# Second self-attention's distance term on VectorE, spatial gate's norm on ScalarE, convolution one step later

## The chip, the cores and the metric
The kernel runs on one core of one Trainium2 chip. The metric is the time of one execution in microseconds (us) on the device: the median of three runs of the kernel before is 791.27 us (791.15 to 791.55). TensorE does the matrix products, VectorE and ScalarE the elementwise work, GpSimd some small work and a few loads, and SyncE issues the weight loads.

## The reference
Two transformer layers on 256 tokens of width 1024, in fp32. The second one holds what is changed:

```
h = rms_norm(x, pre_mix_g);  za, zb, zc = split(h @ w_in)
ya = spatial_gating(gelu(za)):
     u, v = halves;  v = layer_norm(v, ln_g, ln_b)
     mixed[t] = sum_s tril(w_s)[t, s] * v[s] + b_s[t]      (4 heads of 64, chunks of 128 tokens)
     ya = u * mixed
yb = attention of 8 heads of 64: softmax(q.k / 8 - slope_h * (t - s)), causal, slope_h = 2^-(h+1), h = 0..7
yc = silu(group_norm(causal depthwise convolution of 31 taps of a * sigmoid(g)))
x = x + rms_norm(concat(ya, yb, yc) @ w_out, post_mix_g)
```
After it come a cross attention to 256 memory tokens and a feed-forward block. (256 tokens are one block of the block-sparse attention, so all keys up to the query's own are used.)

## The kernel before
**Units.** All weights come in 248 units of 256 rows by 512 columns (512 KB), in a ring of four. For each unit ScalarE makes a rounded high part (`hi`, line 538), VectorE the rest as a low part (`lo`, line 1004), and TensorE multiplies in three passes (lines 1847 to 1849, 1912 to 1915). `after(u)` on ScalarE and VectorE prepares unit u + 4; the high part waits until TensorE has ended unit u and so freed the slot. Each engine's program is written out by hand, in order, and the engines meet at semaphores; nothing is reordered.

**The stretch of the change.** After the first layer's feed-forward block the units come in this order: MEM_K0 (memory keys), GLU2 (convolution input), Q2, K2 (queries and keys), MEM_K1 (2 units), GELU2 (gate, 4), V2 (values, 4), MEM_V0 (memory values, 4), OUT2 (output projection, 8), MEM_V1. The small work of attention, gate and convolution is hung between the units from MEM_K1 on: `follow(step)` exists on TensorE, ScalarE and VectorE, step 0 and 1 are the MEM_K1 units, 2 to 5 GELU2, 6 to 9 V2, 10 to 13 MEM_V0, 14 to 21 OUT2. On TensorE a step's work comes after its unit; on ScalarE after the `after` of its unit; on VectorE ahead of it.

**Attention.** Four pairs of heads, scores at steps 0, 1, 6 and 7. Each pair has two banks. `scores` (line 2112) makes the products of queries and keys (line 2117) and then, in the second attention, adds the distance term by four more products per pair: a diagonal of slopes times the matrix of negative distances with the mask in it (line 2122). `take_maxima` on VectorE reduces the banks (line 1157) and negates (1161); `exponentials` on ScalarE reads the banks (line 612) in the following step; `reciprocals` on VectorE (line 1166) and `normalize` on ScalarE (line 621) follow; `turn_prob` transposes on TensorE (line 2145) at steps 4, 5, 11 and 13. The first attention uses `take_scores` instead: VectorE adds a scalar and a mask to the bank and writes SBUF (line 1141), then takes the maxima there (1148).

**Spatial gate.** `gate_norm` (step 8, VectorE, line 1483) takes the row statistics, GpSimd the power, `gate_scale` (step 9, VectorE, lines 1492 to 1495) subtracts, scales, and applies the norm's weight and bias rows, six instructions of 256 columns. TensorE mixes at step 12 (line 2411), VectorE adds the bias row b_s (line 1504), multiplies by u and splits.

**Convolution.** 62 taps on VectorE (line 1471) are spread behind the units from Q2 on; then TensorE averages over the groups (`conv_center`, step 13), VectorE subtracts, ScalarE squares (13), TensorE sums (14), VectorE copies (14), GpSimd takes the power, TensorE spreads the scale (16), VectorE multiplies (16), ScalarE does Silu (17), VectorE splits into high and low part (18). OUT2's units use the attention's first half (units 0, 1), the gate (2, 3), the attention's second half (4, 5) and the convolution (6, 7: they wait for `yc`).

**Ahead of feed-forward one.** `turn_normed` transposes the normalised rows of token tile 0 and 1, with the two units MEM_KE between.

Of the kernel before, what the change touches and what calls it, by code (L numbers as in the profile page):

```python
# [32 lines left out]
SMALL_LOADS = 7  # L33
# [3 lines left out]
           ("conv_gn_g_2", 2), ("conv_gn_b_2", 2))  # L37
# [4 lines left out]
W_DW, W_CONV, C_POOL, C_BDW, C_GNG, C_GNB = (COL_AT[n] for n in (  # L42
    "w_dw_2", "conv_w", "pool_scale", "b_dw_2", "conv_gn_g_2", "conv_gn_b_2"))
# [206 lines left out]
class Signals:  # L250


    def __init__(self, new):
# [18 lines left out]
        self.ones_ok, self.slopes_ok = new("ones_ok"), new("slopes_ok")  # L272
# [37 lines left out]
        self.gate_var, self.gate_rstd, self.v_normed = new("gate_var"), new("gate_rstd"), new("gate_v_normed")  # L310
        self.gate_mix_ps, self.gate_mixed, self.ya = new("gate_mix_ps"), new("gate_mixed"), new("ya")
# [10 lines left out]
class Memory:  # L322


    def __init__(self, nc, ctx):
# [40 lines left out]
        self.slopes = sb("slope_diagonals", [NH, P], F32R)  # L366
        self.dist_r = sb("neg_dist_rounded", [S], F32R)
# [23 lines left out]
        self.ln_rows = sb("gate_ln_rows", [2, 256])  # L391
# [134 lines left out]
def act_program(nc, t, m, s):  # L526
# [79 lines left out]
    def exponentials(a, g, soft, b=None):  # L606
        act.wait_ge(*a.max.at(g + 1))
        _, negmx, rsum = m.pair_stats(g)
        for e, tt, c0, c1 in parts():
            i = 2 * e + tt  # L610
            logits = soft[:, e, c0:c1] if b is None else bank[b + e][:, c0:c1]
# [218 lines left out]
    act.wait_ge(s.ident_ok, 1)  # L830
    act.wait_ge(s.dist_ok, 1)
# [22 lines left out]
    def follow(step):  # L854
        a = s.att2
        if step == 9:
            normalize(a, 2, m.soft2[2])
        if step in (1, 2, 8, 9):
            g = (1, 2, 8, 9).index(step)
            exponentials(a, g, m.soft2[g], pair_bank(g))  # L860
# [132 lines left out]
def dve_program(nc, m, s):  # L993
# [141 lines left out]
    def take_scores(a, g, b0, b1, soft):  # L1135

        dve.wait_ge(*a.scores.at(g + 1))
        mx, negmx, _ = m.pair_stats(g)
        for e, tt, c0, c1 in parts():
            keys = slice(P, S) if tt == 0 else slice(0, S)  # L1140
            ins = dve.scalar_tensor_tensor(out=soft[:, e, c0:c1], in0=bank[b1 if e else b0][:, c0:c1],
                                           scalar=m.cum8[:, tt, 2 * g + e:2 * g + e + 1], in1=m.mask[:, keys],
                                           op0=ALU.add, op1=ALU.add)
# [6 lines left out]
        dve.tensor_scalar(negmx, mx, -0.125, None, ALU.mult).then_inc(a.max.sem, 1)  # L1150

    def take_maxima(a, g, b):

        dve.wait_ge(*a.scores.at(g + 1))
        mx, negmx, _ = m.pair_stats(g)
        for tt, (c0, c1) in enumerate(CUTS):
            ins = dve.tensor_reduce(mx.rearrange("p (e t) -> p e t", t=NT)[:, :, tt], m.banks[:, b:b + 2, c0:c1], AX.X,
                                    ALU.max)
        ins.then_inc(a.logits.sem, 1)
        dve.wait_ge(*a.logits.at(g + 1))  # L1160
        dve.tensor_scalar(negmx, mx, -0.125, None, ALU.mult).then_inc(a.max.sem, 1)
# [100 lines left out]
    def attention1(step):  # L1262
        if step == 1:
            rows = slice(0, 2 * NH)
            dve.wait_ge(s.cum_ps, 1)
            dve.wait_ge(s.consts_ok, 1)
            dve.tensor_scalar(m.cum8[:, :, :].rearrange("p a h -> p (a h)"), bank[6][:, 0:2 * NH], -1.0, None,
                              ALU.mult).then_inc(s.cum_out, 1)
            own.then(dve.tensor_copy(m.key_round[rows, :], bank[7][rows, 0:S]))
            dve.scalar_tensor_tensor(out=m.key_sums[rows, :], in0=as_f32(m.key_round[rows, :]),  # L1270
                                     scalar=m.low_rows[rows, :], in1=bank[7][rows, 0:S], op0=ALU.mult,
                                     op1=ALU.add).then_inc(s.key_sums, 1)
            dve.wait_ge(s.cum_out, 1)
            dve.wait_ge(s.mask_ok, 1)
        for g, at in enumerate(ATT1_AT):
            if step == at:
                take_scores(s.att1, g, 4, 5, m.soft1[g])
            if step == at + 2:
                reciprocals(s.att1, g)
# [92 lines left out]
    keys_lo(0, 4)  # L1372

# [101 lines left out]
    for j in range(2 * RING):  # L1475
        after(Q2 + j)
        conv_taps(5)

# [9 lines left out]
    def gate_scale():  # L1488
        dve.wait_ge(s.gate_rstd, 1)
        for tt in range(NT):  # L1490
            v = m.vg[:, tt, :]
            own.then(dve.tensor_scalar(v, v, m.gate_stat[:, 2 * tt:2 * tt + 1], m.gate_stat[:, 6 + tt:7 + tt],
                                       ALU.subtract, ALU.mult))
            own.then(dve.tensor_tensor(v, v, m.ln_rows[:, 0, :], ALU.mult))
            dve.tensor_tensor(v, v, m.ln_rows[:, 1, :], ALU.add).then_inc(s.v_normed, 1)
            dve.wait_ge(s.v_normed, tt + 1)

    def gate_mix():
        dve.wait_ge(s.gate_mix_ps, 1)
        dve.wait_ge(s.u_ok, 1)  # L1500
        for tile in range(2):
            for tt in range(NT):
                c = slice(tt * P, tt * P + P)
                ins = dve.tensor_tensor(m.ya[:, tile, c], bank[2][:, tile * S + tt * P:tile * S + tt * P + P],
                                        m.bs_row[:, tile, :], ALU.add)
# [8 lines left out]
    def follow(step):  # L1514
        a = s.att2
        if step in (0, 1, 6, 7):
            g = (0, 1, 6, 7).index(step)
            take_maxima(a, g, pair_bank(g))
# [4 lines left out]
        if step == 9:  # L1523
            gate_scale()
# [9 lines left out]
        if step == 13:  # L1534
            dve.wait_ge(s.conv_mean_ps, 1)
            dve.tensor_tensor(conv2, conv2, bank[5][:, :], ALU.subtract).then_inc(s.conv_cen, 1)
        if step == 14:
            dve.wait_ge(s.conv_var_ps, 1)
            dve.tensor_copy(stat[:, 8:16], bank[5][:, 0:8]).then_inc(s.conv_var, 1)
        if step == 16:  # L1540
            dve.wait_ge(s.conv_scale_ps, 1)
            dve.tensor_tensor(conv2, conv2, bank[5][:, :], ALU.mult).then_inc(s.conv_scaled, 1)
        if step == 18:
# [4 lines left out]
    for j in range(2):  # L1548
        follow(j)
        after(MEM_K1 + j)  # L1550
        conv_taps(1)
    for j in range(RING):
# [4 lines left out]
        conv_taps(4)  # L1557
    for j in range(RING):
# [4 lines left out]
        conv_taps((1, 1, 1, 0)[j])  # L1563
    for j in range(RING):
        follow(10 + j)
        after(MEM_V0 + j)
        conv_taps((1, 0, 0, 0)[j])
# [83 lines left out]
def pool_program(nc, t, m, s):  # L1651
# [94 lines left out]
    load_small(m.ln_rows[:, 0, :], t["gate_ln_g_2"].broadcast_to([P, 256]))  # L1746
    load_small(m.ln_rows[:, 1, :], t["gate_ln_b_2"].broadcast_to([P, 256]))
# [86 lines left out]
def pe_program(nc, m, s):  # L1834
# [277 lines left out]
    def scores(a, g, banks, forget=False):  # L2112


        for e, tt, c0, c1 in parts():
            rows = slice(64 * e, 64 * e + 64)
            mm = pe.matmul(bank[banks[e]][:, c0:c1], m.qT[rows, g, tt * P:tt * P + P], m.kT[rows, g, 0:c1 - c0],  # L2117
                           start=tt == 0, stop=False, skip_group_check=True)
        if forget:
            return  # L2120
# [228 lines left out]
    def early_keys(tt):  # L2349
# [4 lines left out]
        if tt:  # L2354
            free[2] = s.mem_keys, 1

# [33 lines left out]
    def scores2(g):  # L2390
        claim(*pair_banks(g))
        if g == 0:
            pe.wait_ge(s.q2_out, 2)
            pe.wait_ge(s.k2_out, 2)
            pe.wait_ge(s.slopes_ok, 1)
# [49 lines left out]
    def follow(step):  # L2445
# [12 lines left out]
        if step == 13:  # L2458
            conv_center()
        if step == 14:  # L2460
            conv_norm()
        if step == 16:
# [173 lines left out]
```

## Time and profile before
| | |
|---|---|
| median of 3 runs | 791.27 us |
| profiled execution | 791.54 us, span 790.1 us |
| TensorE busy | 775.7 us, 98% |
| VectorE busy | 567.8 us, 72% |
| ScalarE busy | 434.8 us, 55% |
| GpSimd busy | 87.9 us, 11% |
| TensorE's share of the chain that ended last | 91% |

The profile is one execution. Busy time is the share of the span in which an engine had an instruction running. TensorE's products are pipelined, so one of 395 ns is followed by the next after 230 ns; in the chain of waits each stands with the time until the next. The chain follows back from the last instruction to what released each step.

### The profile page before, as it was taken

What the parts mean: (1) busy time and instruction counts of PE and PEld (TensorE: products, weight loads), DVE (VectorE), ACT (ScalarE), POOL (GpSimd) and SP (SyncE); (2) the same over time, 40 slices, a digit from 0 to 9 for tenths busy, and PEclk for the clock granted to TensorE, in tenths of its full rate; (3) what the DMA queues carried; (4) which work ended last, traced back from release to release, by engine and by line L of the source; (5) the groups of instructions that cost most, each with busy time, mean ns of one, the idle gap of its engine ahead of it and who ended that gap; (6) DMA issues with size and microseconds to landing.
All of it is one profiled execution on the core that took longest, in us unless ns stands there. A gap on an engine that the chain in (4) does not pass through costs nothing.

```text
span 790.1 us, 11526 instructions
## 1 busy us (share of the span) xinstructions
PE 775.7 (98%) x4516; PEld 675.0 (85%) x4516; DVE 567.8 (72%) x754; ACT 434.8 (55%) x653; POOL 87.9 (11%) x141
## 2 busy tenths in 40 slices
PE   6999999999999999999999999999999999999997
PEld 5999877788898888888899997889988988888885
DVE  4986999859787567676667997657657666665664
ACT  5555477675665444444466476656646644444452
POOL 5033990000010000000020000101001100000001
PEclk9999999999999999999999999999999999999999
DMA  9998988954457686865556654446433766666651
GB/s 320 367 285 311 359 293 287 349 163 161 133 162 238 197 300 195 266 216 183 166 185 211 181 159 141 146 148 213 149 95 105 215 199 196 188 188 189 190 179 54
DMA packets 84630, 163.61 MB, mean 207 GB/s; under 512 B 5457, under 2 KB 15889, under 8 KB 84577
## 3 DMA queue, kind: packets, MB, share of 16 engines
q1 hardware_dynamic: 82656, 157.31, 62.0%
q10 hardware_dynamic: 1424, 4.81, 1.6%
q0 software_dynamic: 496, 0.76, 0.4%
q8 instruction: 36, 0.59, 0.3%
q14 instruction: 18, 0.14, 0.0%
HBM read 161.81 MB, written 1.05 MB: 206 GB/s over the span
## 4 chain that ended last, share of the span: by engine, by line
PE 91%; DVE 3%; issue 1%; ACT 1%; DMA 1%; SPq 1%; POOL 1%; ACTq 0%; DVEq 0%; POOLq 0%
PE bank L1847 19%; PE bank L1848 19%; PE bank L1849 19%; PE bank L1912 13%; PE bank L1915 7%; PE bank L1860 2%; PE bank L1866 2%; PE bank L1862 2%; DVE ada_acc L1034 1%; DMA raw_ring<-in_w_in 1%; PE bank L1965 1%; PE bank L2540 1%; PE bank L2117 1%; SPq L492 1%; DVE lo_ring L1004 1%
## 5 line engine op out<-in xcount | busy, mean ns | idle before, releaser
L1004 DVE TENSOR_TENSOR lo_ring<-raw_ring,hi_ring 128x1024 fp32r<-128x1024 f32 x248 | 305.6, 1237 | 152.1 <-ACT hi_ring L538 151.4
L538 ACT CAST hi_ring<-raw_ring 128x1024 fp32r<-128x1024 f32 x248 | 259.6, 1052 | 248.8 <-PE bank L1849 148.8
L1847 PE MATMUL bank<-hi_ring,branch_hi 128*128 128x512 f32 x352 | 139.0, 395 | 0.0
L1848 PE MATMUL bank<-lo_ring,branch_hi 128*128 128x512 f32 x352 | 137.2, 390 | 0.0
L1849 PE MATMUL bank<-hi_ring,branch_lo 128*128 128x512 f32 x352 | 137.0, 389 | 0.0
L1912 PE MATMUL bank<-h_hi_lo,hi_ring 128*128 128x512 f32 x448 | 111.8, 391 | 0.0
L1912 PEld LDWEIGHTS bank<-h_hi_lo,hi_ring 128*128 128x128 f32 x448 | 81.3, 189 | 15.1
L1849 PEld LDWEIGHTS bank<-hi_ring,branch_lo 128*128 128x128 f32 x352 | 66.1, 188 | 14.0
L1847 PEld LDWEIGHTS bank<-hi_ring,branch_hi 128*128 128x128 f32 x352 | 66.2, 188 | 13.9 <-issue 0.8
L1848 PEld LDWEIGHTS bank<-lo_ring,branch_hi 128*128 128x128 f32 x352 | 66.2, 188 | 13.4 <-issue 0.5
L1847 PE MATMUL bank<-h_hi_lo,hi_ring 128*128 128x256 f32 x240 | 69.0, 288 | 0.0
L1848 PE MATMUL bank<-h_hi_lo,hi_ring 128*128 128x256 f32 x240 | 67.9, 283 | 0.0
L1849 PE MATMUL bank<-h_hi_lo,lo_ring 128*128 128x256 f32 x240 | 67.9, 283 | 0.0
L1915 PEld LDWEIGHTS bank<-h_hi_lo,lo_ring 128*128 128x128 f32 x448 | 61.1, 190 | 4.4
L1847 PE MATMUL bank<-hi_ring,h_hi_lo 128*128 128x512 f32 (+1 forms) x160 | 63.5, 397 | 0.4 <-DVE post_rows L1112 0.4
L1915 PE MATMUL bank<-h_hi_lo,lo_ring 128*128 128x256 f32 x448 | 62.5, 282 | 0.0
L1849 PE MATMUL bank<-hi_ring,h_hi_lo 128*128 128x512 f32 (+1 forms) x160 | 60.9, 380 | 0.0
L1848 PE MATMUL bank<-lo_ring,h_hi_lo 128*128 128x512 f32 (+1 forms) x160 | 60.8, 380 | 0.0
L1683 POOL TENSOR_SCALAR stat<-stat 128x1 f32<-128x1 f32 x10 | 2.6, 261 | 440.5 <-ACT gates L597 440.5
L1847 PEld LDWEIGHTS bank<-h_hi_lo,hi_ring 128*128 128x128 f32 x240 | 46.0, 192 | 0.4 <-issue 0.2
L1848 PEld LDWEIGHTS bank<-h_hi_lo,hi_ring 128*128 128x128 f32 x240 | 46.0, 192 | 0.2
L1849 PEld LDWEIGHTS bank<-h_hi_lo,lo_ring 128*128 128x128 f32 x240 | 46.0, 191 | 0.0
(301 smaller groups left out, 1179.3 us busy)
## 6 DMA issues: line engine op xcount, KB each, us to landing
raw_ring<-in_w_ff SPq DMA_DIRECT2D x128, 512.0 KB, 3.7
raw_ring<-in_w_in SPq DMA_DIRECT2D x64, 512.0 KB, 4.6
raw_ring<-in_w_out SPq DMA_DIRECT2D x16, 512.0 KB, 3.4
raw_ring<-in_w_xkv SPq DMA_DIRECT2D x16, 512.0 KB, 3.6
mem_v<-in_w_ada SPq DMA_DIRECT2D x13, 512.0 KB, 5.3
mem_k<-in_w_ada SPq DMA_DIRECT2D x11, 512.0 KB, 4.9
ada_ring<-in_w_ada SPq DMA_DIRECT2D x8, 512.0 KB, 6.9
raw_ring<-in_w_branch SPq DMA_DIRECT2D x8, 512.0 KB, 3.8
```

What stands on the lines that cost most here:

```text
L492: sp.dma_start(dst[:, :, i * S:i * S + S] if a < ADA_FIRST else dst.rearrange("p k n -> p (k n)"), src).then_inc(s.ada_in[slot], DMA)
L538: act.copy(m.hi[:, m.slot(u)], m.raw[:, m.slot(u)]).then_inc(s.hi_done, 1)
L1004: dve.tensor_tensor(m.lo[:, m.slot(u)], m.raw[:, m.slot(u)], as_f32(m.hi[:, m.slot(u)]), ALU.subtract).then_inc(s.lo_done, 1)
L1034: ins = dve.scalar_tensor_tensor(out=acc, in0=w, scalar=m.silu_c[:, kc:kc + 1], in1=acc, op0=ALU.mult, op1=ALU.add)
L1847: pe.matmul(out, a_hi, b_hi, start=start, stop=False, skip_group_check=True)
L1848: pe.matmul(out, a_hi, b_lo, start=False, stop=False, skip_group_check=True)
L1849: return pe.matmul(out, a_lo, b_hi, start=False, stop=stop, skip_group_check=True)
L1860: pe.matmul(out, m.hi[:, slot, k, fc], x_hi[:, k0 + k, :], start=first and k == 0 and f % 2 == 0, stop=False, skip_group_check=True)
L1862: pe.matmul(out, m.lo[:, slot, k, fc], x_hi[:, k0 + k, :], start=False, stop=False, skip_group_check=True)
L1866: mm = pe.matmul(bank[banks[f // 2]][:, (f % 2) * S:(f % 2) * S + S], m.hi[:, slot, k, fc], x_lo[:, k0 + k, :], start=False, stop=last and ...
L1912: pe.matmul(b, m.hi[:, slot, k, fc], x_both[:, k0 + k].rearrange("p a s -> p (a s)"), start=first and k == 0, stop=False, skip_group_check ...
L1915: mm = pe.matmul(b[:, 0:S], m.lo[:, slot, k, fc], x_both[:, k0 + k, 0, :], start=False, stop=last and k == UK - 1, skip_group_check=True)
```

## The change
In words: the second attention's scores are no longer completed by TensorE. `take_scores` gets a second form, in which VectorE multiplies the negative distances (with the mask) by the head's slope, adds the bank, writes SBUF, and takes the maxima there; ScalarE's exponentials read SBUF; the banks are free once VectorE has read them. The slope diagonals and the rounded distances go. The gate's norm is split: VectorE computes a shift (minus mean times the inverse deviation), ScalarE applies scale and shift at step 10, the norm's weight multiplies behind the mix, and the norm's bias comes in through the row sums of w_s, which TensorE makes ahead of feed-forward one and VectorE folds into the b_s rows. The norm's weight and bias come with the column load instead of two row loads on GpSimd's queue. The convolution's steps from `conv_center` on move one step later, and its taps are spread otherwise. The scratch for software DMA goes back to its default size.

```diff
 take_scores, second form (VectorE), instead of take_maxima
+                slope = 2.0 ** (-8.0 * (2 * g + e + 1) / NH)
+                ins = dve.scalar_tensor_tensor(out=soft[:, e, c0:c1], in0=m.dist[:, keys], scalar=8.0 * slope, in1=src,
+                                               op0=ALU.mult, op1=ALU.add)
...
-            take_maxima(a, g, pair_bank(g))
+            take_scores(a, g, pair_bank(g), pair_bank(g) + 1, m.soft2[g], False)
 scores (TensorE)
-        for e, tt, c0, c1 in parts():
-            mm = pe.matmul(bank[banks[e]][:, c0:c1], m.slopes[:, 2 * g + e, :], m.dist_r[:, P if tt == 0 else 0:],
-                           start=False, stop=True, skip_group_check=True)
-        mm.then_inc(a.scores.sem, 1)
-        free[banks[0]] = free[banks[1]] = a.exp.at(g + 1)
+        if not forget:
+            scored(a, g, banks, mm)
 ScalarE, after gain_hi(s.in2t, ...)
-    for h in range(NH):
-        act.activation(m.slopes[:, h, :], m.ident[:, :], ACT.Copy, scale=8.0 * 2.0 ** (-8.0 * (h + 1) / NH))
-    act.copy(m.dist_r[:, :], m.dist[:, :]).then_inc(s.slopes_ok, 1)
 exponentials (ScalarE)
-            ins = act.activation(soft[:, e, c0:c1], logits, ACT.Exp, bias=negmx[:, i:i + 1], scale=0.125,
+            ins = act.activation(soft[:, e, c0:c1], soft[:, e, c0:c1], ACT.Exp, bias=negmx[:, i:i + 1], scale=0.125,
 follow (ScalarE)
+        if step == 10:
+            act.wait_ge(s.gate_shift, 1)
+            for tt in range(NT):
+                v = m.vg[:, tt, :]
+                act.activation(v, v, ACT.Identity, bias=m.gate_stat[:, 4 + tt:5 + tt],
+                               scale=m.gate_stat[:, 6 + tt:7 + tt]).then_inc(s.v_normed, 1)
-        if step == 13:
+        if step == 14:
             act.wait_ge(s.conv_cen, 1)
-        if step == 17:
+        if step == 18:
             act.wait_ge(s.conv_scaled, 1)
 VectorE: gate_scale becomes gate_shift; gate_mix
+        dve.scalar_tensor_tensor(out=m.gate_stat[:, 4:6], in0=mean, scalar=-1.0, in1=m.gate_stat[:, 6:8], op0=ALU.mult,
+                                 op1=ALU.mult).then_inc(s.gate_shift, 1)
...
-                ins = dve.tensor_tensor(m.ya[:, tile, c], bank[2][...], m.bs_row[:, tile, :], ALU.add)
+                ins = dve.scalar_tensor_tensor(out=m.ya[:, tile, c], in0=bank[2][...],
+                                               scalar=cols[:, C_LNG + tile:C_LNG + tile + 1], in1=m.bs_row[:, tile, :], ...)
 VectorE, ahead of feed-forward one, after keys_lo(0, 4)
+    dve.wait_ge(s.ws_sums, 1)
+    for tile in range(2):
+        ins = dve.scalar_tensor_tensor(out=row, in0=bank[3][:, tile * P:tile * P + P], scalar=..., in1=row, ...)
+    ins.then_inc(s.gate_rows, 1)
 early_keys (TensorE), after the second MEM_KE unit
+            claim(3)
+            pe.wait_ge(s.wsT_ok, 1)
+            for h in range(4):
+                mm = pe.matmul(bank[3][...], m.ones[:, 0:64], m.ws_T[:, h, :], start=True, stop=True)
+            mm.then_inc(s.ws_sums, 1)
+            free[3] = s.gate_rows, 1
 VectorE's convolution: steps 13, 14, 16, 18 become 14, 15, 17, 19; TensorE's 13, 14, 16 become 14, 15, 17; taps
-        conv_taps(1)                          (MEM_K1, each of 2)
-        conv_taps(4)                          (GELU2)
+        conv_taps((4, 4, 3, 3)[j])
-        conv_taps((1, 1, 1, 0)[j])            (V2)
+        conv_taps((0, 1, 3, 1)[j])
-        conv_taps((1, 0, 0, 0)[j])            (MEM_V0)
+        conv_taps((2, 1, 0, 0)[j])
```

## Rows read from the trace of the kernel before
**Rows 1.** Busy time by stretch: stretch, length, engines with instructions, TensorE clock, DMA.
```profile
396.00:527.00 131.00, 131.00 (x922) 117.92 (x921) 99.71 (x165) 79.89 (x146) 9.76 (x14) 1.00 0.53 166
527.00:560.00 33.00, 33.00 (x218) 30.27 (x217) 22.86 (x29) 21.86 (x37) 3.16 (x9) 1.00 0.61 192
```
**Rows 2.** Chain of waits, distance products of first and last pair: start, us, what.
```profile
457.24 0.66 PE bank L2122 x4
...
483.00 0.65 PE bank L2122 x4
```
**Rows 3.** Timeline of TensorE, third turn: start, us, engine line op, count.
```profile
494.40 0.82 PE L2145 MATMUL bank<-ident,gates 128*128 128x128 f32 x6
```
**Rows 4.** Timeline of VectorE, first pair of the second attention.
```profile
459.67 1.01 DVE L1157 TENSOR_REDUCE softmax_stats<-bank 128x2 f32<-128x256 f32 x2
...
460.79 1.22 DVE L1004 TENSOR_TENSOR lo_ring<-raw_ring,hi_ring 128x1024 fp32r<-128x1024 f32 x1
```
**Rows 5.** Timeline of VectorE, a pair of the first attention.
```profile
128.79 1.38 DVE L1141 SCALAR_TENSOR_TENSOR softmax<-bank,cum_log_f,mask 128x128 f32<-128x128 f32 x4
...
131.45 1.22 DVE L1004 TENSOR_TENSOR lo_ring<-raw_ring,hi_ring 128x1024 fp32r<-128x1024 f32 x1
```
**Rows 6.** Timeline of VectorE, low part, taps, keys, reciprocal; row statistics.
```profile
466.41 1.23 DVE L1004 TENSOR_TENSOR lo_ring<-raw_ring,hi_ring 128x1024 fp32r<-128x1024 f32 x1 [1.24 <-ACT hi_ring L538]
467.55 1.67 DVE L1471 SCALAR_TENSOR_TENSOR mix<-pad_u,vector_columns,mix 128x256 f32<-128x256 f32 x4
469.13 0.68 DVE L1093 TENSOR_TENSOR mem_k_lo<-bank,mem_k_hi 128x512 fp32r<-128x512 f32 x1
469.74 0.17 DVE L1166 RECIPROCAL softmax_stats<-softmax_stats 128x4 f32<-128x4 f32 x1
...
486.36 0.42 DVE L1483 BATCH_NORM_STATS2 bn_stats<-mix 128x6 f32<-128x256 f32 x1
...
487.70 1.23 DVE L1004 TENSOR_TENSOR lo_ring<-raw_ring,hi_ring 128x1024 fp32r<-128x1024 f32 x1
```
**Rows 7.** Timeline of ScalarE, second normalise to the end of the Gelus.
```profile
470.16 1.53 ACT L621 ACTIVATE gates<-gates,softmax_stats 128x128 f32<-128x128 f32 x4
471.56 1.07 ACT L538 CAST hi_ring<-raw_ring 128x1024 fp32r<-128x1024 f32 x1
472.50 0.83 ACT L626 COPY gates<-bank 128x768 f32<-128x768 f32 x1
473.34 1.28 ACT L892 ACT_TABLE_LOAD   x1
...
475.66 1.06 ACT L538 CAST hi_ring<-raw_ring 128x1024 fp32r<-128x1024 f32 x1
```
**Rows 8.** Timeline of TensorE, ahead of feed-forward one; the gate's mix.
```profile
225.22 1.09 PE L1965 MATMUL bank<-ident,gates 128*128 128x128 f32 x8 [0.55 <-DVE gates L1054]
...
499.47 1.09 PE L2411 MATMUL bank<-w_s_T,mix 128*64 128x128 f32 x14
```
**Rows 9.** Timelines of TensorE, ScalarE, VectorE, OUT2's units 4 to 6.
```profile
520.60 0.39 PE L1847 MATMUL bank<-hi_ring,branch_hi 128*128 128x512 f32 x1
...
526.04 0.39 PE L1847 MATMUL bank<-hi_ring,branch_hi 128*128 128x512 f32 x1
...
520.86 1.05 ACT L538 CAST hi_ring<-raw_ring 128x1024 fp32r<-128x1024 f32 x1 [2.92 <-PE bank L1849]
521.92 1.28 ACT L878 ACT_TABLE_LOAD   x1
523.22 1.09 ACT L878 ACTIVATE mix<-mix,vector_columns 128x256 f32<-128x256 f32 x2
...
524.80 0.69 DVE L1177 TENSOR_TENSOR branch_lo<-mix,branch_hi 128x512 fp32r<-128x512 f32 x1
```
**Rows 10.** Timeline of TensorE, the kernel's first products.
```profile
5.62 3.75 PE L2032 MATMUL bank<-x_residual,ones 128*128 128x256 f32 x8 [5.62 <-DMA x_residual<-in_x]
...
12.16 2.76 PE L2032 MATMUL bank<-x_residual,ones 128*128 128x256 f32 x12
```

More of the change, by code:

```diff
@@ L41 @@
     "mem_g_2", "g_mix_pre", "b_ada", "g_ff_pre", "pre_mix_g_2", "pre_x_g_2", "pre_ffn_g_2"))
-W_DW, W_CONV, C_POOL, C_BDW, C_GNG, C_GNB = (COL_AT[n] for n in (
-    "w_dw_2", "conv_w", "pool_scale", "b_dw_2", "conv_gn_g_2", "conv_gn_b_2"))
+W_DW, W_CONV, C_POOL, C_BDW, C_GNG, C_GNB, C_LNG, C_LNB = (COL_AT[n] for n in (
+    "w_dw_2", "conv_w", "pool_scale", "b_dw_2", "conv_gn_g_2", "conv_gn_b_2", "gate_ln_g_2", "gate_ln_b_2"))
 FIRST, MIX_B, GATES = 0, 16, 20
@@ L604, in post_squares, with exponentials @@
             post_square(post, n, tt, banks[tt])
-    def exponentials(a, g, soft, b=None):
+    def exponentials(a, g, soft):
         act.wait_ge(*a.max.at(g + 1))
@@ L859, in follow @@
             g = (1, 2, 8, 9).index(step)
-            exponentials(a, g, m.soft2[g], pair_bank(g))
+            exponentials(a, g, m.soft2[g])
         if step in (2, 3):
@@ L1139, in take_scores @@
         for e, tt, c0, c1 in parts():
+            src = bank[b1 if e else b0][:, c0:c1]
             keys = slice(P, S) if tt == 0 else slice(0, S)
-            ins = dve.scalar_tensor_tensor(out=soft[:, e, c0:c1], in0=bank[b1 if e else b0][:, c0:c1],
-                                           scalar=m.cum8[:, tt, 2 * g + e:2 * g + e + 1], in1=m.mask[:, keys],
-                                           op0=ALU.add, op1=ALU.add)
+            if forget:
+                ins = dve.scalar_tensor_tensor(out=soft[:, e, c0:c1], in0=src,
+                                               scalar=m.cum8[:, tt, 2 * g + e:2 * g + e + 1], in1=m.mask[:, keys],
+                                               op0=ALU.add, op1=ALU.add)
+            else:
+                slope = 2.0 ** (-8.0 * (2 * g + e + 1) / NH)
+                ins = dve.scalar_tensor_tensor(out=soft[:, e, c0:c1], in0=m.dist[:, keys], scalar=8.0 * slope, in1=src,
+                                               op0=ALU.mult, op1=ALU.add)
         ins.then_inc(a.logits.sem, 1)
@@ L1149, in take_scores @@
         own.then(ins)
[L1150 to L1160, printed above, removed]
         dve.tensor_scalar(negmx, mx, -0.125, None, ALU.mult).then_inc(a.max.sem, 1)
@@ L1372, in dve_program @@
     keys_lo(0, 4)
+    dve.wait_ge(s.ws_sums, 1)
+    dve.wait_ge(s.small_in, SMALL_LOADS * DMA)
+    for tile in range(2):
+        row = m.bs_row[:, tile, :]
+        ins = dve.scalar_tensor_tensor(out=row, in0=bank[3][:, tile * P:tile * P + P],
+                                       scalar=cols[:, C_LNB + tile:C_LNB + tile + 1], in1=row, op0=ALU.mult, op1=ALU.add)
+    ins.then_inc(s.gate_rows, 1)
     def gate_row(step, q):
@@ L1477, in dve_program @@
         conv_taps(5)
+    dve.wait_ge(s.dist_ok, 1)
     def gate_norm():
@@ L1486, in gate_norm, with gate_shift @@
             dve.wait_ge(s.gate_var, tt + 1)
-    def gate_scale():
+    def gate_shift():
         dve.wait_ge(s.gate_rstd, 1)
[L1490 to L1496, printed above, removed]
+        mean = m.gate_stat[:, 0:4].rearrange("p (a b) -> p a b", b=2)[:, :, 0]
+        dve.scalar_tensor_tensor(out=m.gate_stat[:, 4:6], in0=mean, scalar=-1.0, in1=m.gate_stat[:, 6:8], op0=ALU.mult,
+                                 op1=ALU.mult).then_inc(s.gate_shift, 1)
     def gate_mix():
         dve.wait_ge(s.gate_mix_ps, 1)
+        dve.wait_ge(s.gate_rows, 1)
         dve.wait_ge(s.u_ok, 1)
@@ L1503, in gate_mix @@
                 c = slice(tt * P, tt * P + P)
-                ins = dve.tensor_tensor(m.ya[:, tile, c], bank[2][:, tile * S + tt * P:tile * S + tt * P + P],
-                                        m.bs_row[:, tile, :], ALU.add)
+                ins = dve.scalar_tensor_tensor(out=m.ya[:, tile, c], in0=bank[2][:, tile * S + tt * P:tile * S + tt * P + P],
+                                               scalar=cols[:, C_LNG + tile:C_LNG + tile + 1], in1=m.bs_row[:, tile, :],
+                                               op0=ALU.mult, op1=ALU.add)
         ins.then_inc(s.gate_mixed, 1)
@@ L1523, in follow @@
         if step == 9:
-            gate_scale()
+            gate_shift()
         if step == 12:
@@ L2117, in scores @@
             mm = pe.matmul(bank[banks[e]][:, c0:c1], m.qT[rows, g, tt * P:tt * P + P], m.kT[rows, g, 0:c1 - c0],
-                           start=tt == 0, stop=False, skip_group_check=True)
-        if forget:
-            return
-        for e, tt, c0, c1 in parts():
-            mm = pe.matmul(bank[banks[e]][:, c0:c1], m.slopes[:, 2 * g + e, :], m.dist_r[:, P if tt == 0 else 0:],
-                           start=False, stop=True, skip_group_check=True)
-        mm.then_inc(a.scores.sem, 1)
-        free[banks[0]] = free[banks[1]] = a.exp.at(g + 1)
+                           start=tt == 0, stop=not forget, skip_group_check=True)
+        if not forget:
+            scored(a, g, banks, mm)
     def scored(a, g, banks, mm):
@@ L2355, in early_keys @@
             free[2] = s.mem_keys, 1
+            claim(3)
+            pe.wait_ge(s.wsT_ok, 1)
+            for h in range(4):
+                mm = pe.matmul(bank[3][64 * (h % 2):64 * (h % 2) + 64, h // 2 * P:h // 2 * P + P], m.ones[:, 0:64],
+                               m.ws_T[:, h, :], start=True, stop=True)
+            mm.then_inc(s.ws_sums, 1)
+            free[3] = s.gate_rows, 1
     turn_normed(s.ff1t, early_keys)
@@ L2457, in follow @@
             gate_mix()
-        if step == 13:
+        if step == 14:
             conv_center()
-        if step == 14:
+        if step == 15:
             conv_norm()
-        if step == 16:
+        if step == 17:
             conv_silu()
```

34 lines of the change are left out of this document (11 added, 23 removed).

## The prediction
> **What bounds the kernel now.** I read the busy times by stretch first: from 396 to 560 us, which holds everything that the change touches but the four small products in front of the first feed-forward block, TensorE is busy 131.00 of 131.00 and 33.00 of 33.00 us [rows 1]. It is never kept waiting there, so what counts is only TensorE's own work and any wait that the change opens. The chain of waits has the products that are to go as pieces of its own [rows 2]: they lie on the path that sets the end. Only then did I go to the timelines of VectorE and ScalarE, because time taken from an engine that never waits is kept only if its helpers keep up [rows 3 to 7].
>
> **Distance products off TensorE.** Per pair of heads four products of the slope diagonals go, 0.66 us a pair, first pair at 457.24, last at 483.00 [rows 2]; four pairs make 2.63 us. Nothing hides them, so all of it comes off unless a wait opens. The eight slope copies and the rounding of the distances on ScalarE go as well; TensorE never waits near them [rows 1], so they count nothing.
>
> **Distance term on VectorE.** Before, a pair costs VectorE two maxima from PSUM and a negation, 459.67 to 460.79, 1.12 us [rows 4]. After, it is the sequence of the first attention: four scalar_tensor_tensor, four maxima, a negation, 128.79 to 131.45, 2.66 us [rows 5]. So each pair costs VectorE 1.54 us more. The form itself (distance in SBUF first, bank second, an immediate scalar) is not in the trace. From below it is bounded by the old 1.12 us; from above by 3.16 us, all eight as dear as a tap of 256 columns (0.395) [rows 6], though half of them have 128. I take 2.66, since operations, shapes and the PSUM operand are those of rows 5.
>
> VectorE comes to the first pair straight from the taps, without a gap, at 459.67, when the pair's products have been done since 457.90 [rows 2, 4]: a faster TensorE doesn't bring it there earlier. From there I add up in program order, with low parts of 1.14, taps of 0.395 (four in 1.58, 467.55 to 469.13), the memory keys' low part 0.68, a reciprocal 0.17 [rows 6]:
> 459.67 + 2.66 + 1.14 + 2.66 + 1.14 (both pairs, two low parts; the taps that stood here have moved) + 0.10 (first reciprocal) + 1.14 + 1.58 + 0.68 + 0.17 = 470.94, the second pair's reciprocal.
> ScalarE waits for that, then runs normalise 1.40, high part 0.94, copy of the turned pair 0.84, table load with the three Gelus 2.32, high part 1.06 [rows 7]: with 0.05 for the hand-over 477.55.
> VectorE takes that high part: low part 1.14, three taps 1.19, third pair 2.66, low part 1.14, fourth pair 2.66, low part 1.14, one tap 0.40, the two row statistics 1.34 [rows 6], low part 1.14, three taps 1.19, then the third pair's reciprocal 0.17: 491.77. Normalise to the last piece adds 1.40 and some 0.2 of end and hand-over: TensorE can turn the third pair at 493.4. Before, it did so at 494.40 [rows 3]. Without waits it would be there at 494.40 - 2.63 = 491.8, so it stands still for 1.6 us and 1.0 us of the gain is left. Both ends: at the old 1.12 a pair VectorE would be early and nothing lost; at 3.16 (0.5 more, four times) the wait is 2.0 us longer and the change is 1.0 behind at this point. Smaller waits at the first two turns would be a part of this loss, not more: the third turn is set by VectorE, not by when TensorE comes. Behind the reciprocal on VectorE stand the gate's statistics-to-shift step, the value copy and a low part; none is needed by TensorE before the turn.
>
> **Layer norm on ScalarE.** VectorE loses six instructions over 256 columns and gets one tiny one; ScalarE gets two of 256 columns, at most the 1.40 us of four in rows 7. The loss of VectorE's six comes behind the reciprocal that is late, so it does not help the third turn. ScalarE's two stand in front of the copy of the third turned pair; in ScalarE's queue behind it come that copy, the fourth normalise, two high parts and two attended tiles, which the fourth pair's turn needs; between the two turns TensorE has two units of 2.72 us and the products of attention and mix. The exponentials read SBUF, not PSUM, which is no larger change than a piece. I take 0; ends 0 and 0.4. The mix's four additions become scalar_tensor_tensor, a little dearer each: VectorE only, and TensorE next needs their result two units later.
>
> **Row sums ahead of feed-forward one.** Four fp32 products of 128 columns are eight passes; 14 such passes in the mix take 1.09 us with their tail [rows 8], about 0.06 a pass, so 0.5 us. They stand where TensorE waits for VectorE's scaled rows: 0.55 us idle at 225.22 [rows 8]. I take 0.03; ends 0 and 0.5. VectorE's two scaled sums follow the keys' low part, with TensorE in its leading units for 2 us more. The two loads that go from GpSimd's queue and the wider column load: 0, TensorE waits for none of them.
>
> **Convolution one step later.** The taps keep their number (62). The centring, norm, scaling and Silu each move behind one later unit of the output projection, but the consumer does not: units 6 and 7 need the convolution's output. Before: unit 4 starts at 520.60, which is when unit 3 has ended and ScalarE is let into its high part at 520.86; table load 521.92, Silu 523.22, VectorE's second half at 524.80 for 0.69, done 525.49; TensorE wants it at 526.04 [rows 9]. Slack 0.55. ScalarE's high part stands in front of the Silu in its queue and waits for a unit's end, so after the change all this hangs on the end of unit 4, one unit (5.44 / 2 = 2.72 us) later, while unit 6 comes no later. The wait: 2.72 - 0.55 + 0.1 hand-over = 2.27 us. It is independent of what was gained or lost earlier, as both ends hang on the same unit. Ends: 2.0 and 2.5. What follows (squares of the projection, memory values) hangs on the units and moves with them.
>
> A rule of the Trainium skill speaks against such stalls. The row first: granted clock 1.00 (2.4 GHz) in this whole stretch, with no idle time in it [rows 1]; at the kernel's start, after 5.62 us idle, eight products take 3.75 us, 0.47 each, and later twelve alike 2.76, 0.23 each, as at half clock and at full [rows 10]. "TensorE: Matmul & The Clock Gate", part 1, has it that TensorE falls back to half its clock when idle and that activity releases it. No run here shows whether 2.27 us idle is enough; by the rule the sum would be larger by the price of the second rival.
>
> **Sum.** -2.63 + 1.6 + 0 + 0.03 + 2.27 = +1.27; I take +1.2 (the hand sum of some twenty steps is rounded up at each). The profiled execution took 791.54 us (span 790.1), so 792.7 for it; the median of the runs shown is 791.27, 0.27 less, so I forecast 792.5. A measurement of this kernel can tell 0.2% (1.6 us) from no change: +1.2 is within it.
>
> **Rivals.** *Kept gain*: the third turn is not late (a take nearer 2.2 us), only the convolution's wait is there: -2.63 + 2.27 = -0.4, 790.9. For it: the slack of a long sum; against: VectorE's four pairs are 6.2 us dearer and only four taps move out from between the pairs and the reciprocal. *Clock falls* (the other side; the page named above states such a fall): in the wait ahead of unit 6 the granted clock drops to 1.2 GHz; the first eight products of rows 10 took 3.75, at full clock 8 x 2.76 / 12 = 1.84, so one such recovery is 1.9 us: +3.1, 794.4. It decides from the point where 2 us of idle drop the clock; idle of 0.55 us did not. *Dearer take* (the other side too): VectorE's form takes 2.86 or more a pair, four times 0.2: +2.0, 793.3; from 2.76 a pair the change is measurably slower. Rows 5 stand against it; that the operands are swapped stands for it. *Convolution not late*: if something lets the Silu off the high part, -1.0 to -2.63, 788.6 to 790.3; the queue's order speaks against it. *The change doesn't do what it says*: TensorE's removed time is certain, so this would only be the two stalls absent, the case just named.
>
> **Numbers.** Forecast 0.60 (of which 0.05 lies over +1.6), kept gain 0.08, clock 0.09, dearer take 0.20, convolution not late 0.03. Slower by over 0.2%: 0.09 + 0.20 + 0.05 = 0.34 less some 0.04 of dearer takes that stay under it: 0.30. Faster by over 0.2%: 0.03. Same: 0.67. Range: from the kept gain to the middle between the dearer take and the clock, 790.9 to 793.9.
>
> **What would show it.** Right: TensorE idle some 1 to 1.7 us in front of the third turn, with ScalarE's normalise waiting for VectorE's reciprocal; 2.0 to 2.5 us idle in front of unit 6 of the output projection, released by VectorE; takes of 2.66 us. Wrong: no idle time at one of the two places, a granted clock under 1.00 behind them, or a wait in front of the first feed-forward block over 0.7 us.

## The result and the profile after

The changed kernel takes 793.18 us (median of 12 runs, 791.89 to 793.74) against 791.10 us of the kernel before (12 runs, 790.92 to 791.55): ratio 1.0025, 95% interval 1.0017 to 1.0033. It is 2.1 us slower. That is inside the predicted range, 0.7 us above the predicted time, and a little over the 1.6 us that the prediction called no change. The profiled execution has a span of 791.9 us (before 790.1), TensorE busy 776.1 us, VectorE 570.6, ScalarE 434.7.

Of the waits of TensorE on other engines, one is new and large. The columns are: waiting line, releaser, total us, times, longest.

```profile
PE bank L2028 <- DMA x_residual<-in_x: 5.4, 1, 5.4
PE bank L1843 <- DVE branch_lo L1170: 2.1, 1, 2.1
PE bank L2147 <- ACT prob_T L623: 0.7, 1, 0.7
```

It is the wait ahead of unit 6 of the output projection. No wait stands at the third turn (it would be released by ScalarE's normalise, line 618). The busy times around the wait have the columns of [rows 1]:

```profile
520.00:527.00 7.00, 4.93 (x21) 3.71 (x20) 3.54 (x5) 4.36 (x5) 0.00 (x0) 0.95 0.45 151
527.00:532.00 5.00, 5.00 (x18) 4.02 (x17) 0.72 (x2) 1.23 (x4) 0.19 (x1) 0.73 0.32 105
532.00:540.00 8.00, 8.00 (x43) 6.78 (x42) 7.28 (x11) 5.72 (x11) 1.87 (x5) 1.00 0.38 133
```

The reader is to see the clock: 1.00 (2.4 GHz) everywhere here before [rows 1], now 0.73 on average behind the wait, and 1.00 again from 532 on. TensorE's timeline shows it product by product (last two of unit 5, first three and the tenth of unit 6, first of unit 7, first of the memory values):

```profile
523.42 0.39 PE L1844 MATMUL bank<-lo_ring,branch_hi 128*128 128x512 f32 x1
523.64 0.39 PE L1845 MATMUL bank<-hi_ring,branch_lo 128*128 128x512 f32 x1
526.10 0.65 PE L1843 MATMUL bank<-hi_ring,branch_hi 128*128 128x512 f32 x1 [2.06 <-DVE branch_lo L1170]
526.54 0.63 PE L1844 MATMUL bank<-lo_ring,branch_hi 128*128 128x512 f32 x1
526.97 0.63 PE L1845 MATMUL bank<-hi_ring,branch_lo 128*128 128x512 f32 x1
...
529.84 0.40 PE L1843 MATMUL bank<-hi_ring,branch_hi 128*128 128x512 f32 x1
...
530.54 0.39 PE L1843 MATMUL bank<-hi_ring,branch_hi 128*128 128x512 f32 x1
...
533.26 0.39 PE L1843 MATMUL bank<-hi_ring,memT_hi 128*128 128x512 f32 x1
```

Ahead of the wait the products start 0.22 to 0.23 us apart; behind it eight start 0.42 to 0.44 apart, as at 1.2 GHz, and the ninth 0.31. Unit 6 lasts 4.44 us from its first product to that of unit 7. Without a wait a unit lasts 2.72; behind the same wait with the clock at 1.00 unit 6 lasts 2.86 (experiment 5). So the clock costs 1.58 us in this execution, and 0.14 us belongs to the wait even where the clock holds.

Where the time went is read from starts of the same product in both profiled executions (negative: the changed kernel is earlier):

| point | before | after | difference |
|---|---|---|---|
| second turn ahead of feed-forward one | 225.22 [rows 8] | 224.90 | -0.32 |
| third turn | 494.40 [rows 3] | 492.24 | -2.16 |
| unit 5 of the output projection | 523.32 | 521.15 | -2.17 |
| unit 6 | 526.04 [rows 9] | 526.10 | +0.06 |
| unit 7 | 528.76 | 530.54 | +1.78 |
| span | 790.1 | 791.9 | +1.8 |

The first 0.32 us was there before anything changed (the first load arrived 0.2 us earlier, for one). The change gains 1.84 up to the third turn, loses 2.23 in the wait ahead of unit 6 and 0.14 behind it, and 1.58 to the clock.

### The profile page after: what moved, and what is told of

The parts are those of the page before. It is cut to its first block, busy times and chain, and to the rows that moved or that the text cites. A ratio compares the mean times of both kernels' runs of the same rounds, so it can differ in the third digit from the quotient of the medians.

```text
span 791.9 us, 11523 instructions
## 1 busy us (share of the span) xinstructions
PE 776.1 (98%) x4508; PEld 674.4 (85%) x4508; DVE 570.6 (72%) x775; ACT 434.7 (55%) x646; POOL 86.6 (11%) x139
## 4 chain that ended last, share of the span: by engine, by line
PE 92%; DVE 3%; ACT 2%; issue 1%; DMA 1%; SPq 1%; POOL 0%; ACTq 0%; DVEq 0%; POOLq 0%
PE bank L1843 20%; PE bank L1844 19%; PE bank L1845 19%; PE bank L1908 13%; PE bank L1911 7%; PE bank L1856 2%; PE bank L1862 2%; PE bank L1858 2%; DVE ada_acc L1032 1%; PE bank L1961 1%; DMA raw_ring<-in_w_in 1%; PE bank L2537 1%; PE bank L2113 1%; SPq L490 1%; DVE lo_ring L1002 1%
```

## The experiments

All times are medians of 5 to 11 runs beside the kernel before on the same chip; three chips were used, and the kernel before took 791.43 to 791.47 us on them. With the intervals of the ratio:

| kernel | us | ratio to before |
|---|---|---|
| convolution's steps back | 789.35 | 0.9974 (0.9965 to 0.9984) |
| Silu and split first | 789.49 | 0.9975 (0.9965 to 0.9984) |
| distance term and taps only | 789.58 | 0.9975 (0.9966 to 0.9985) |
| distance term only | 790.00 | 0.9982 (0.9973 to 0.9991) |
| Silu first | 790.61 | 0.9990 (0.9981 to 0.9999) |
| slope in a column | 790.76 | 0.9991 (0.9982 to 1.0000) |
| third turn late | 790.87 | 0.9994 (0.9985 to 1.0003) |
| norm only | 791.41 | 1.0000 (0.9991 to 1.0008) |
| wait filled | 791.92 | 1.0006 (0.9997 to 1.0015) |
| changed kernel again | 793.22 | 1.0018 (1.0010 to 1.0027) |
| late convolution only | 794.00 | 1.0035 (1.0023 to 1.0048) |
| late convolution only, again | 794.09 | 1.0038 (1.0026 to 1.0051) |

**1. The convolution's steps back.** The theory: the late convolution is the whole loss.

```diff
 VectorE; the same on TensorE (14, 15, 17 become 13, 14, 16) and ScalarE (14, 18 become 13, 17)
-        if step == 14:   # subtract the mean
+        if step == 13:
...
-        if step == 19:   # split the Silu
+        if step == 18:
```

> The changed kernel with the convolution's steps at their old places on all three engines (13, 14, 16 on TensorE; 13, 17 on ScalarE; 13, 14, 16, 18 on VectorE); distance term, norm and taps as changed. Theory A (the late convolution is the whole loss: a wait of 2.4 us ahead of unit 6 of the output projection and 1.7 us of half clock behind it): no wait there, granted clock 1.00 to the end, 793.2 - 4.1 = 789.1 us, about 2 us under the kernel before. Rival B (the wait comes from VectorE or ScalarE being fuller in general, wherever the convolution stands): a wait of over 1 us stays ahead of unit 6, 791 us or more. Rival C (the prediction's sum: a wait at the third turn of 1.6 us is left): TensorE idle there, some 790.

789.35 us, granted clock 1.00 in the profile, no wait at either place. Rivals B and C fall: the rest of the change gains 2.1 us and keeps it.

**2. The late convolution alone,** on the kernel before, run twice.

```diff
 VectorE, and the same on TensorE and ScalarE
-        if step == 18:
+        if step == 19:
```

> The kernel before with only the convolution's steps one later; distance term, norm and taps as before. Theory A (wait and clock fall belong to this part alone): wait of 2.4 us ahead of unit 6, half clock behind it worth 1.7 us, 791.1 + 4.1 = 795.2 us. The prediction's price without a fall of the clock: 791.1 + 2.3 = 793.4. Rival B (the part costs only beside the fuller VectorE): under 792.

> The kernel before with only the convolution late, once more, for the share of executions in which the clock falls behind the same 2.06 us of idle time. Theory A (rarer here than in the changed kernel): median 794.0 us, a few runs at 795.4 with mean clock 0.996. Rival B (it goes by the chip): the same share as the changed kernel beside it.

794.00 and 794.09 us, 2.6 us over the kernel before. The wait is the same to the hundredth, but in this profile the clock stays:

```profile
525.83 0.39 PE L1849 MATMUL bank<-hi_ring,branch_lo 128*128 128x512 f32 x1
528.28 0.50 PE L1847 MATMUL bank<-hi_ring,branch_hi 128*128 128x512 f32 x1 [2.06 <-DVE branch_lo L1177]
528.62 0.40 PE L1848 MATMUL bank<-lo_ring,branch_hi 128*128 128x512 f32 x1
```

Seven of the ten runs lie at 793.77 to 794.11 with a mean clock of 0.998 to 0.999, three at 795.36 to 795.56 with 0.996. (A mean of 0.998 is no sign of a fall here: in this profile the clock is 1.00 up to 785 us and 0.80 in the last 7.5.) So the wait belongs to this part alone, as theory A says; that it always halves the clock is wrong.

**3. Silu first; Silu and split first.** TensorE's convolution products stay late; only places in two queues change.

```diff
 ScalarE, output projection (both kernels)
+        if i == 4:
+            follow(14 + i)
         after(OUT2 + i)
-        follow(14 + i)
+        if i != 4:
+            follow(14 + i)
 VectorE (second kernel only)
-        if step == 19:   # split the Silu
+        if step == 18:
```

> The changed kernel with one thing moved: at unit 4 of the output projection ScalarE does the Silu ahead of the high part instead of behind it. VectorE's split of the Silu keeps its late place behind the low part. Theory A (ScalarE's queue order makes most of the wait): Silu done by 520.8 instead of 524.9; VectorE's split then stands behind its low part, which ends at 523.6, so the first product of unit 6 waits 0.9 us instead of 2.4. If so short a wait leaves the clock alone: 793.2 - 1.5 - 1.7 = 790.0 us; if it too halves the clock: 791.7. Rival B (the convolution's own chain, not the queue, is late): wait unchanged, 793.2.

> As the kernel with the Silu first, and VectorE's split of the Silu also one step earlier, ahead of the low part; TensorE's convolution products and the centring stay one step late. Theory A (only the two places in the queues cost, the late products are free): no wait ahead of unit 6, granted clock 1.00, 789.1 us, the same as with all the convolution's steps back. Rival B (the late products themselves cost): 790 to 793.

790.61 and 789.49 us. With the Silu ahead of the high part the wait shrinks to what VectorE's low part leaves, and the clock holds:

```profile
524.78 0.50 PE L1846 MATMUL bank<-hi_ring,branch_hi 128*128 128x512 f32 x1 [0.80 <-DVE branch_lo L1173]
525.12 0.40 PE L1847 MATMUL bank<-lo_ring,branch_hi 128*128 128x512 f32 x1
```

With the split moved too, no wait is left, and the time is that of experiment 1 within 0.2 us. The late products on TensorE cost nothing; what cost was the Silu behind a high part, and the split behind a low part, each of which waits for a unit's end.

**4. The wait filled.**

```diff
 TensorE, output projection, ahead of pe.wait_ge(s.yc, 1)
+            if i == 6:
+                claim(5)
+                for _ in range(8):
+                    pe.matmul(bank[5][:, :], ..., start=True, stop=True)
```

> The changed kernel with eight products of 512 columns into a bank that nobody reads, issued by TensorE just ahead of its wait for the convolution's output at unit 6; they add nothing to the result. At 0.23 us each they fill 1.8 of the 2.4 us. Theory A (idle time makes the clock fall): the wait for the output ends at the same time, granted clock 1.00 behind it, units 6 and 7 start 2.72 us apart, 793.2 - 1.7 = 791.5 us. Rival B (the fall has another cause, such as what the other engines do there): units 6 and 7 still 4.4 us apart, 793.2.

791.92 us (791.70 to 792.09). The output comes as late as before, but the idle time is 0.26 us and no product behind it is slow:

```profile
524.23 1.98 PE L2492 MATMUL bank<-branch_hi 128*128 128x512 f32 x8
526.46 0.50 PE L1843 MATMUL bank<-hi_ring,branch_hi 128*128 128x512 f32 x1 [0.26 <-DVE branch_lo L1170]
526.79 0.40 PE L1844 MATMUL bank<-lo_ring,branch_hi 128*128 128x512 f32 x1
```

VectorE and ScalarE run the same instructions there as in the changed kernel, and the clock held in all 11 runs, where the unfilled kernel kept it in 6 of 23 (experiment 5). So the clock falls behind idle time, not behind what the other engines do. One reservation: the unfilled kernel did not run on the chip of this experiment, and its runs on others stand in for it. The wait alone, without the clock, is 791.92 - 789.35 = 2.6 us by medians.

**5. The changed kernel again,** unedited.

> The changed kernel itself, beside the late convolution alone on the same chip. Theory A (2.06 us of idle time sits where the clock falls in some executions and not in others, more often here than with the late convolution alone): mean granted clock 0.996 to 0.997 in most runs, median 793.2 us. Rival B (the share of executions in which it falls goes by the chip): clock as with the late convolution alone, and the times 2.3 to 2.6 us apart from the kernel with the steps back where it doesn't fall, 791.9.

Its runs fall into two groups: four at 791.97 to 792.12 with a mean clock of 0.999, seven at 793.16 to 793.83 with 0.996. The profile taken this time is of the first group:

```profile
524.11 0.39 PE L1845 MATMUL bank<-hi_ring,branch_lo 128*128 128x512 f32 x1
526.56 0.50 PE L1843 MATMUL bank<-hi_ring,branch_hi 128*128 128x512 f32 x1 [2.07 <-DVE branch_lo L1170]
526.90 0.39 PE L1844 MATMUL bank<-lo_ring,branch_hi 128*128 128x512 f32 x1
...
529.42 0.39 PE L1843 MATMUL bank<-hi_ring,branch_hi 128*128 128x512 f32 x1
```

The last line is unit 7's first product: unit 6 lasts 529.42 - 526.56 = 2.86 us. One program, one wait, the clock at 0.5 behind it or not. Where it held, the changed kernel is 0.6 us slower than the kernel before (792.02 against 791.43), where it fell 1.9 (793.33): the 2.1 us of the result depend on how often it falls. The groups are 1.3 us apart, less than the 1.58 of the one execution read above; why is not known. The 12 runs of the result divide alike: ten with 0.996 or 0.997, two (791.89, 792.04) with more. Together the clock fell in 17 of 23 executions of the changed kernel and in 3 of 10 of experiment 2. On one chip, in this set, it was 7 of 11 against 2 of 5, too few to say that the two kernels differ.

**6. The distance term only; distance term and taps only; norm only.** Parts of the change on the kernel before.

```diff
 distance term (first two kernels)
-            take_maxima(a, g, pair_bank(g))
+            take_scores(a, g, pair_bank(g), pair_bank(g) + 1, m.soft2[g], False)
 taps (second kernel)
-        conv_taps(1)                          (MEM_K1)
-        conv_taps(4)                          (GELU2)
+        conv_taps((4, 4, 3, 3)[j])
...
 norm (third kernel)
-            gate_scale()
+            gate_shift()
```

> The kernel before with only the distance term moved to VectorE; norm, convolution and taps as before, so that VectorE has three taps (1.2 us) more ahead of the third pair's reciprocal than in the changed kernel. Theory A (TensorE's gain is 0.46 us a pair, 1.8 in all, and in the changed kernel the third turn had about 0.4 us to spare): a wait of 0.8 us in front of the third turn, 791.1 - 1.8 + 0.8 = 790.1 us. The prediction's prices (2.63 of gain, takes of 2.66 us): a wait of 2.8 us there, 791.1 - 2.6 + 2.8 = 791.3. Rival B (takes never decide, no wait at all): 789.3.

> The kernel before with the distance term on VectorE and the taps spread as in the change; the gate's norm and the convolution's steps as before. Theory A (the norm's part is worth nothing, the taps' spread is worth the 0.35 us of wait at the third turn that the distance term alone left): no wait there, 789.4 us, as with the convolution's steps back. Rival B (VectorE needs the norm's part off it to keep up): a wait of 0.3 us or more stays, 789.8 to 790.0.

> The kernel before with only the gate's norm changed (scale and shift on ScalarE, weight behind the mix, row sums of w_s ahead of feed-forward one, two loads fewer); distance term, convolution and taps as before. Theory A (all of it beside TensorE's work, the row sums inside the 0.55 us wait): 791.1 us, within 0.2. Rival B (the row sums are not hidden): 791.6. Rival C (ScalarE's two extra instructions make the fourth turn late): up to 0.4 us idle there, 791.5.

790.00, 789.58 and 791.41 us. The distance term alone leaves a small wait at the third turn:

```profile
492.86 0.85 PE L2128 MATMUL bank<-ident,gates 128*128 128x128 f32 x6 [0.35 <-ACT gates L618]
```

With the taps spread as in the change it is gone, and the 0.4 us with it; so that edit earns its place, and the norm is worth nothing either way. The 0.35 us is half of the 0.8 expected. The distance term with the taps is as fast as experiment 1 with less changed.

**7. The third turn made late,** to see whether the predicted mechanism is there at all.

```diff
 experiment 1, taps of VectorE
-        conv_taps((0, 1, 3, 1)[j])            (V2)
+        conv_taps((0, 3, 5, 0)[j])
-        conv_taps((2, 1, 0, 0)[j])            (MEM_V0)
+        conv_taps((0, 0, 0, 0)[j])
```

> The kernel with the convolution's steps back, and with the last four taps (1.58 us) moved ahead of the third pair's reciprocal on VectorE; the number of taps is the same. Theory A (the predicted mechanism at the third turn is real, and the changed kernel only had 0.4 us to spare): a wait of 1.1 to 1.2 us in front of the third turn, ScalarE's normalise released by VectorE's reciprocal, 789.1 + 1.15 = 790.2 us if the clock stays, about 1.7 more if it falls. Rival B (the third turn does not hang on that reciprocal): no wait, 789.1.

790.87 us, 1.5 over experiment 1 (expected 1.15). VectorE's reciprocal, ScalarE's normalise behind it, and TensorE's turn behind that:

```profile
491.99 0.17 DVE L1159 RECIPROCAL softmax_stats<-softmax_stats 128x4 f32<-128x4 f32 x1
```
```profile
492.19 1.49 ACT L618 ACTIVATE gates<-gates,softmax_stats 128x128 f32<-128x128 f32 x4 [1.91 <-DVE softmax_stats L1159]
```
```profile
493.83 0.85 PE L2136 MATMUL bank<-ident,gates 128*128 128x128 f32 x6 [1.14 <-ACT gates L618]
```

The chain is the predicted one, and 1.58 us of work opened 1.14 us of idle time. From start to start the third turn comes 268.63 us behind the second turn ahead of feed-forward one, where experiment 1 and the changed kernel have 267.34: it is 1.29 us late, and they had 0.3 us to spare. The granted clock behind this idle time was 1.00.

**8. The slope in a column.** A take measured 2.41 us where the prediction had 2.66; this asks why.

```diff
 experiment 1, VectorE (GpSimd fills the column at the start)
-                ins = dve.scalar_tensor_tensor(out=soft[:, e, c0:c1], in0=m.dist[:, keys], scalar=8.0 * slope, in1=src,
+                ins = dve.scalar_tensor_tensor(out=soft[:, e, c0:c1], in0=m.dist[:, keys],
+                                               scalar=m.slope8[:, 2 * g + e:2 * g + e + 1], in1=src,
```

> The kernel with the convolution's steps back, in which VectorE's distance term reads the head's slope from a column of 128 values (one per partition) instead of having it as an immediate number; operand order and everything else stay. Theory A (the immediate is why a take measured 2.41 us against the first attention's 2.66): takes of 2.66 us, 0.25 more for each of four, 1.0 us in all ahead of the third reciprocal, of which 0.4 was spare: a wait of 0.6 us in front of the third turn, 789.35 + 0.6 = 789.95 us. Rival B (the order of the operands is why): takes stay at 2.41 us, no wait, 789.35.

The instruction grouped by shape (busy us, mean ns), first experiment 1, then the column:

```profile
L1146 DVE SCALAR_TENSOR_TENSOR gates<-neg_dist,bank 128x256 f32<-128x256 f32 x8 | 3.3, 410 | 0.0
L1146 DVE SCALAR_TENSOR_TENSOR gates<-neg_dist,bank 128x128 f32<-128x128 f32 x8 | 2.2, 276 | 0.0
```
```profile
L1146 DVE SCALAR_TENSOR_TENSOR gates<-neg_dist,slope_column,bank 128x256 f32<-128x256 f32 x8 | 3.8, 475 | 0.0
L1146 DVE SCALAR_TENSOR_TENSOR gates<-neg_dist,slope_column,bank 128x128 f32<-128x128 f32 x8 | 2.7, 342 | 0.0
```

Some 65 ns more in either shape, so it is a price per instruction; with the column a take is 2.66 us again, as in [rows 5]. The third turn waits 0.52 us, near the 0.6 expected. The median is 1.4 us up. In the profile the third turn comes 0.67 us later than in experiment 1, counted from the second turn ahead of feed-forward one; another 0.46 stands already at that second turn, before the edited lines run. Whether filling the column causes that was not tried.

## Why the prediction was right and wrong

By its own signs the prediction was wrong at two places: no idle time stands at the third turn, and the granted clock behind unit 6's wait was under 1.00. The number came out near by luck, because errors of both signs met: +0.8 us for the distance products, -1.6 for the third turn, +0.1 for the wait ahead of unit 6, +1.6 for the clock, +0.9 together. Step by step:

- **What bounds the kernel:** right. Only TensorE's own work and the waits that opened changed the time.
- **Distance products, 2.63 us predicted, 1.84 measured: the first step that failed.** The prediction took 0.66 us a pair from the chain of waits [rows 2]. That piece runs to the modelled end of the last product (457.24 + 0.66 = 457.90), but the next unit's first product started before that. Before:

```profile
456.31 0.93 PE L2117 MATMUL bank<-k_T,q_T 64*128 64x128 f32 x8
457.17 0.73 PE L2122 MATMUL bank<-neg_dist_rounded,slope_diagonals 128*128 128x128 f32 x4
457.74 0.29 PE L1847 MATMUL bank<-memT_hi,hi_ring 128*128 128x256 f32 x1
457.87 0.28 PE L1848 MATMUL bank<-memT_lo,hi_ring 128*128 128x256 f32 x1
```

and after:

```profile
455.99 0.93 PE L2113 MATMUL bank<-k_T,q_T 64*128 64x128 f32 x8
456.86 0.38 PE L1843 MATMUL bank<-memT_hi,hi_ring 128*128 128x256 f32 x1
457.08 0.28 PE L1844 MATMUL bank<-memT_lo,hi_ring 128*128 128x256 f32 x1
```

From start to start the four products held TensorE for 457.74 - 457.17 = 0.57 us, and the product that now stands directly behind the 64-row products takes 0.22 instead of 0.13 to the next: 0.47 for this pair. From the starts of the four pairs and of the third turn the gains are 0.47, 0.48, 0.44 and 0.45, 1.84 in all. The Trainium skill, "TensorE: Matmul & The Clock Gate", part 2 (what happens when a matmul is issued), says that the drain of one product overlaps the fill of the next; these rows agree, as far as modelled ends can show it: the next product starts 0.16 us before the end of the four.
- **Takes, 2.66 us predicted, 2.41 measured** (459.35 to 461.76). The row chosen [rows 5] had a scalar from a column, the new form has an immediate; experiment 8 shows that this is the difference.

```profile
459.35 1.14 DVE L1146 SCALAR_TENSOR_TENSOR gates<-neg_dist,bank 128x128 f32<-128x128 f32 x4
...
461.76 1.22 DVE L1002 TENSOR_TENSOR lo_ring<-raw_ring,hi_ring 128x1024 fp32r<-128x1024 f32 x1
```

- **Wait at the third turn, 1.6 us predicted, none measured: the second step that failed,** by its sizes alone. VectorE's reciprocal came at 490.11, where the prediction's sum, set on this execution's 0.32 us earlier start, puts its start at 491.28: 1.2 us earlier, 1.0 of it the four takes. (The terms of that sum add up to 491.72, not 491.77, and three taps moved out ahead of the reciprocal, 21 becoming 18, not four as the rival says; neither changes the reading.) TensorE came 0.8 later than predicted, because it gained less. 1.6 - 1.2 - 0.8 = -0.4, no wait, near the 0.3 to spare of experiment 7. Rival "kept gain" named this outcome; it asked for takes near 2.2 us, but 2.41 was enough with TensorE later.

```profile
490.11 0.17 DVE L1159 RECIPROCAL softmax_stats<-softmax_stats 128x4 f32<-128x4 f32 x1
```
```profile
492.24 0.81 PE L2136 MATMUL bank<-ident,gates 128*128 128x128 f32 x6
```

- **Norm on ScalarE, 0; row sums, 0.03:** right. Experiment 6 gives 791.41 against 791.44. The row sums stand in the former idle time [rows 8], and the two turns are 4.45 us apart before (220.77 and 225.22) and after:

```profile
220.45 1.03 PE L1961 MATMUL bank<-ident,gates 128*128 128x128 f32 x8
224.28 0.66 PE L2350 MATMUL bank<-w_s_T,ones 128*64 128x128 f32 x8
224.90 1.10 PE L1961 MATMUL bank<-ident,gates 128*128 128x128 f32 x8
```

- **Convolution, 2.27 us predicted, 2.23 measured** at unit 6's start and 2.37 with what follows in the unit: right, in size and cause. ScalarE's queue after, against [rows 9]:

```profile
521.41 1.05 ACT L536 CAST hi_ring<-raw_ring 128x1024 fp32r<-128x1024 f32 x1 [2.92 <-PE bank L1845]
522.47 1.28 ACT L876 ACT_TABLE_LOAD   x1
523.77 1.09 ACT L876 ACTIVATE mix<-mix,vector_columns 128x256 f32<-128x256 f32 x2
```

- **Clock: the third step that failed, in its chance.** The rival had 0.09 and 1.9 us; the fall came in 17 of 23 executions and cost 1.58 in the one profiled, and the sum had put it at nothing. The prediction had nothing between 0.55 us idle, which left the clock alone, and 5.62, behind which products came as at half clock [rows 8, 10] (seen from their spacing; the profile has no record of the granted clock that early). With 2.06 lying between, 0.09 was too sure. By the Trainium skill, "TensorE: Matmul & The Clock Gate", part 1, the fall follows idle time, with which experiment 4 agrees. The same part has it that what the chip looks at is not tied to the kernel's start, so that one kernel can fare differently from run to run; the two groups of experiment 5 look like that, but nothing here shows that it is the reason, and it stays open.

Added up in the profiled executions: -0.32 (there beforehand) - 1.84 + 2.23 + 0.14 + 1.58 = +1.8, the difference of the spans. By medians the gain (2.1) is 0.3 larger than from starts, and the wait (2.6) 0.2 larger. Of the gain's surplus 0.2 lies outside the span of the profile: time less span is 1.24 us in experiment 1 and 1.46 in the kernel before (medians), while the kernel with the distance term and the taps only has 1.45 and gains 1.85, as the starts say. With the norm alone it is 1.23, and the span 0.3 longer instead; why is not shown. The wait's surplus is open too.

## What to carry to other kernels

When a step of a side computation is moved later, look in each engine's queue for what it comes to stand behind: here two places behind instructions that wait for a unit's end cost 2.4 us by starts (2.6 by medians) and the moved products themselves nothing. Price work that leaves a pipelined engine from start to start of its neighbours, in the order they will have, not by the length of its pieces. A wait of 2 us on TensorE has to be priced with and without half clock behind it: here filling it with products that nobody reads saved 1.3 us by medians, and avoiding it 3.9.

## What the runs showed of the hardware

- The same 2.06 to 2.07 us of idle time left the granted clock at 1.00 in some executions and took it to 1.2 GHz in others; 0.80 us and 1.14 us left it at 1.00 in the profiles of experiments 3 and 7.
- A wait costs TensorE more than the idle time that the profile shows. Behind 2.06 to 2.07 us with the clock at 1.00, unit 6 started 2.22 us late and then lasted 2.85 to 2.89 instead of 2.72 (three profiles, experiments 2 and 5); behind 1.14 us the third turn came 1.29 late (experiment 7).
- A scalar from a column costs VectorE's scalar_tensor_tensor 65 ns more than an immediate number (276 to 342 ns at 128 columns, 410 to 475 at 256).
